# Split products for the attention and recurrence inputs of the second block's mixer

## The reference

```
x = x + 0.5 * swiglu(rms_norm_2(x, norm_ffn1[l]), ffn1_in[l], ffn1_out[l])
h = rms_norm_2(x, norm_mix[l])
proj = h @ w_in[l]
p_rwkv, p_attn, p_gate = split(proj, [C_RWKV, C_RWKV + C_ATTN])
o_a = rwkv7_mixer(p_rwkv, ...)          # C_RWKV = 1920 columns
o_b = diff_attention(p_attn, ...)       # C_ATTN = 1536 columns: q, k, v
merged = sum(sigmoid(p_gate) * [o_a @ w_branch[0], o_b @ w_branch[1]])
x = x + merged @ w_out[l]
x = x + 0.5 * swiglu(rms_norm_2(x, norm_ffn2[l]), ffn2_in[l], ffn2_out[l])
```

## Time and profile before

| | |
|---|---|
| median of 3 runs | 4137.35 us (4134.38 to 4137.35) |
| the profiled execution | 4137.76 us, of which the span from first to last instruction is 4136.1 us |
| PE | busy 3485.1 us, 84% of the span |
| DVE | 1569.9 us, 38% |
| ACT | 842.4 us, 20% |
| POOL | 599.4 us, 14% |
| mean granted clock of TensorE | 0.890 |

### The profile page before, as it was taken

How to read it: one execution, slowest core, us unless ns; L and a number is a source line. 1 busy time by engine, 2 the same in 40 slices (tenths; PEclk the granted TensorE clock), 3 DMA queues, 4 the chain that set the end, 5 groups by cost and what they waited for, 6 DMA issues and landing times.

```text
span 4136.1 us, 46292 instructions
## 1 busy us (share of the span) xinstructions
PE 3485.1 (84%) x18496; PEld 2414.5 (58%) x18496; DVE 1569.9 (38%) x2703; ACT 842.4 (20%) x1240; POOL 599.4 (14%) x556
## 2 busy tenths in 40 slices
PE   6888999994788899999299958798988994879899
PEld 3754333331566333333098648686978963877688
DVE  4433222224634222222354265531545426554154
ACT  1211111110130111111132221111324223111132
POOL 4402233331440233233100000000000000000000
PEclk8889999997878999999699968779998996877999
DMA  7647999985754899889554300004536430000352
GB/s 264 236 158 279 364 347 354 356 338 197 283 181 168 343 351 353 341 350 358 181 195 153 130 8 1 1 21 147 199 102 225 159 117 21 1 1 13 130 204 102
DMA packets 305420, 799.38 MB, mean 193 GB/s; under 512 B 57030, under 2 KB 155868, under 8 KB 251308
## 3 DMA queue, kind: packets, MB, share of 16 engines
q1 hardware_dynamic: 245804, 727.16, 46.8%
q0 software_dynamic: 58848, 67.05, 4.9%
q10 hardware_dynamic: 544, 2.10, 0.1%
HBM read 989.01 MB, written 53.48 MB: 252 GB/s over the span
## 4 chain that ended last, share of the span: by engine, by line
PE 41%; DVE 6%; ACT 1%; issue 1%; DMA 1%; SPq 0%; DVEq 0%
PE s_bank L1899 12%; PE s_bank L1937 6%; PE s_bank L1887 5%; PE s_bank L2083 2%; PE s_bank L1964 2%; PE s_bank L2098 2%; PE s_bank L2093 1%; PE s_bank L2200 1%; PE s_bank L2210 1%; PE s_bank L2168 1%; PE s_bank L2160 1%; PE s_bank L2071 1%; DMA s_ringA<-in_ffn_in 1%; PE s_bank L2153 1%; PE s_bank L2145 1%
## 5 line engine op out<-in xcount | busy, mean ns | idle before, releaser
L711 PE MATMUL f_bank<-f_ringA,f_arena 128*64 128x512 f32 x3072 | 688.7, 601 | 16.3 <-DMA f_ringA<-in_w_up,f_chosen 10.1
L711 PEld LDWEIGHTS f_bank<-f_ringA,f_arena 128*64 128x64 f32 x3072 | 222.3, 138 | 401.4 <-issue 400.1
L1899 PE MATMUL s_bank<-s_hT_high_parts,s_highA_parts 128*128 128x256 f32 x1408 | 402.7, 286 | 17.7 <-DVE s_hT_parts L2428 17.7
L1899 PE MATMUL s_bank<-s_hT_parts,s_highA_parts 128*128 128x256 f32 x1408 | 402.2, 286 | 0.0
L1899 PE MATMUL s_bank<-s_hT_high_parts,s_ringA_parts 128*128 128x256 f32 x1408 | 402.0, 285 | 0.0
L732 PE MATMUL f_bank<-f_ringB,f_arena 128*64 128x512 f32 x1536 | 346.5, 592 | 1.0 <-DVE f_arena L1473 1.0
L1012 ACT ACTIVATE f_arena<-f_bank 128x512 f32<-128x512 f32 (+1 forms) x362 | 202.1, 587 | 575.1 <-PE f_bank L692 174.2
L1465 DVE TENSOR_TENSOR f_arena<-f_arena,f_bank 128x256 f32<-128x256 f32 x96 | 58.6, 610 | 636.3 <-ACT f_arena L1090 636.3
L1899 PEld LDWEIGHTS s_bank<-s_hT_high_parts,s_highA_parts 128*128 128x128 f32 x1408 | 274.2, 195 | 20.4 <-issue 19.0
L1899 PEld LDWEIGHTS s_bank<-s_hT_parts,s_highA_parts 128*128 128x128 f32 x1408 | 274.3, 195 | 1.4
L1899 PEld LDWEIGHTS s_bank<-s_hT_high_parts,s_ringA_parts 128*128 128x128 f32 x1408 | 274.1, 195 | 0.0
(11 more groups left out here) (393 smaller groups left out, 5361.2 us busy)
## 6 DMA issues: line engine op xcount, KB each, us to landing
f_ringA<-in_w_gate SPq DMA_DIRECT2D x128, 1024.0 KB, 8.7
f_ringA<-in_w_up SPq DMA_DIRECT2D x128, 1024.0 KB, 11.1
f_ringB<-in_w_down SPq DMA_DIRECT2D x128, 1024.0 KB, 12.3
s_ringA<-in_ffn_in SPq DMA_DIRECT2D x88, 1024.0 KB, 7.7
f_ringA<-in_w_ada SPq DMA_DIRECT2D x48, 1024.0 KB, 8.4
s_arena<-in_ffn_out SPq DMA_DIRECT2D x44, 1024.0 KB, 6.0
s_ringA<-in_w_in SPq DMA_DIRECT2D x40, 1024.0 KB, 6.1
f_ringA<-in_w_in SPq DMA_DIRECT2D x28, 1024.0 KB, 10.2
```

Of the source, the lines that this page charges most:

```text
L711: last = mm(ps[j * CAP:(j + 1) * CAP, :].rearrange("p (h c) -> p h c", h=2), picked[:, b % 2, k, j * CAP:(j + 1) * CAP], gu[j][:, :, k, :] ...
L1899: last = mm(ps[:, t * S:(t + 1) * S], parts_of(wx[:, k, cs_]), parts_of(hx[:, k, :]), start=(k == 0 and x == 0), stop=(k == DT - 1 and x = ...
```

## The change

The attention and the recurrence input products of the mixer are formed from high and low parts in three products, in the manner of the feed-forward. The seven chunks that they read (MIX = 7) are copied by ACT (`mix_up`) into the two buffers of `highA` and reduced by DVE (`mix_down`). hT is split as well, with the low part in a place of its own, `hT_low`, since the gates' products still need hT whole. TensorE waits for `mix_low` instead of the landing of a chunk, and at the first product for `mix_split`, the four splits of hT.

```
+        hT_low = parts_of.part("hT_low", arena, arena_at, 20480, 2048).rearrange("p (t s) -> p t s", s=S)
...
+        def mix_chunk(c):
+            width = 512 if c < MIX - 1 else CRW - 1536
+            return [rows8(w)[:, :, 0:width] for w in (slotA(a_at + c), highA[:, (STEPS + c) % 2, :])]
...  TensorE
                 for c in range(3):
-                    landed(a_at + c)
-                    w = rows8(slotA(a_at + c))
+                    pe.wait_ge(mix_low, c + 1)
+                    w, high = mix_chunk(c)
                     for m in range(MT):
                         ps = banks.claim(pe, ("at", c, m))
                         for k in range(DT):
-                            last = mm(ps[:, :], hT[:, k, m * P:(m + 1) * P], w[:, k, :],
-                                      start=(k == 0), stop=(k == DT - 1))
+                            if c == m == 0 and k % 2 == 0:
+                                pe.wait_ge(mix_split, k // 2 + 1)
+                            for x, (hx, wx) in enumerate(((hT_high, high), (hT_low, high), (hT_high, w))):
+                                last = mm(ps[:, :], parts_of(hx[:, k, m * P:(m + 1) * P]), parts_of(wx[:, k, :]),
+                                          start=(k == 0 and x == 0), stop=(k == DT - 1 and x == 2))
                 for g in range(8):
-                    c = a_in + g // 2
                     if g % 2 == 0:
-                        landed(c)
...
+                        pe.wait_ge(mix_low, 3 + g // 2 + 1)
+                    w, high = mix_chunk(3 + g // 2)
...
+                        for k in range(DT):
+                            for x, (wx, hx) in enumerate(((high, hT_high), (high, hT_low), (w, hT_high))):
+                                last = mm(ps[:, t * S:(t + 1) * S], parts_of(wx[:, k, o:o + P]), parts_of(hx[:, k, :]),
...  ACT
+            def mix_up(c):
+                a_filled(act, a_at + c)
+                banks.read(act, ("u", 0, STEPS - 2 + c) if c < 2 else ("at", c - 2, 1) if c < 5 else ("rw", 2 * (c - 5) + 1))
+                w, high = mix_chunk(c)
+                f(parts_of(high), w, ACT.Copy).then_inc(mix_high, 1)
             def norm(k, at):
+                if k == 1:
+                    mix_up(0)
                 if k:
                     act.wait_ge(x_ready, k)
...
                 roots(MT)
+                if k == 1:
+                    mix_up(1)
...
                 for c in range(3):
                     for m in range(MT):
                         take(("at", c, m), at_tok[:, m, c * 512:(c + 1) * 512], lambda ps: ps[:, :])
+                    mix_up(c + 2)
                 act.wait_ge(lam_asked, 1)
...  in the loop over g
+                    if g in (1, 3):
+                        mix_up(5 + g // 2)
...  DVE
+                def mix_down(c):
+                    w, high = mix_chunk(c)
+                    dve.wait_ge(mix_high, c + 1)
+                    tt(parts_of(w), w, parts_of.value(high), ALU.subtract).then_inc(mix_low, 1)
```

More of the change, by code:

```diff
@@ L1640, in second_block @@
         lowB_ready, hT_split, hid_split = each["lowB_ready"], each["hT_split"], each["hid_split"]
+        mix_high, mix_low, mix_split = each["mix_high"], each["mix_low"], each["mix_split"]
         merged, dve_steps, arrived = each["merged"], each["dve_steps"], each["arrived"]
@@ L1963, in _ @@
                         for k in range(DT):
-                            last = mm(ps[:, :], hT[:, k, m * P:(m + 1) * P], w[:, k, :],
-                                      start=(k == 0), stop=(k == DT - 1))
+                            if c == m == 0 and k % 2 == 0:
[3 more added lines that the diff above has]
+                                          start=(k == 0 and x == 0), stop=(k == DT - 1 and x == 2))
                         banks.fill(last, ("at", c, m))
                 for g in range(8):
-                    c = a_in + g // 2
                     if g % 2 == 0:
-                        landed(c)
-                    w = rows8(slotA(c))
+                        pe.wait_ge(mix_low, 3 + g // 2 + 1)
+                    w, high = mix_chunk(3 + g // 2)
                     ps = banks.claim(pe, ("rw", g))
-                    o = (g % 2) * 2 * P
-                    banks.fill(hidden(ps, w[:, :, o:o + 2 * P], 1 if g == 7 else 2), ("rw", g))
+                    for t in range(1 if g == 7 else 2):
+                        o = (2 * (g % 2) + t) * P
+                        for k in range(DT):
+                            for x, (wx, hx) in enumerate(((high, hT_high), (high, hT_low), (w, hT_high))):
+                                last = mm(ps[:, t * S:(t + 1) * S], parts_of(wx[:, k, o:o + P]), parts_of(hx[:, k, :]),
+                                          start=(k == 0 and x == 0), stop=(k == DT - 1 and x == 2))
+                    banks.fill(last, ("rw", g))
                 pe.wait_ge(at_ready, 1)
@@ L2266, in norm @@
                         j = 2 * b + t
[L2267 to L2270 removed]
+                        f(hT[:, j, :], ps[:, t * S:(t + 1) * S], ACT.Copy, scale=cols[:, at + j:at + j + 1])
+                        last = f(parts_of(hT_high[:, j, :]), ps[:, t * S:(t + 1) * S], ACT.Copy,
+                                 scale=cols[:, at + j:at + j + 1])
                     banks.free(last, key)
@@ L2410, in norm @@
                         split_up(k, 0)
+                    else:
+                        mix_down(1)
                     if k == 0:
@@ L2417, in norm @@
                             j = 2 * b + t
-                            last = ts(hT[:, j, :], ps[:, t * S:(t + 1) * S], cols[:, at + j:at + j + 1], None,
-                                      ALU.mult)
-                            if k != 1:
-                                last = ts(parts_of(hT_high[:, j, :]), ps[:, t * S:(t + 1) * S],
-                                          cols[:, at + j:at + j + 1], None, ALU.mult)
-                        banks.free(last, key)
-                    if k != 1:
-                        for b in range(4):
-                            banks.evacuated(dve, ("xT", k, b))
-                            two = slice(2 * b, 2 * b + 2)
-                            tt(parts_of(hT[:, two, :]), hT[:, two, :], parts_of.value(hT_high[:, two, :]),
-                               ALU.subtract).then_inc(hT_split, 1)
+                            ts(hT[:, j, :], ps[:, t * S:(t + 1) * S], cols[:, at + j:at + j + 1], None,
+                               ALU.mult)
+                            last = ts(parts_of(hT_high[:, j, :]), ps[:, t * S:(t + 1) * S],
+                                      cols[:, at + j:at + j + 1], None, ALU.mult)
+                        banks.free(last, key)
+                    for b in range(4):
+                        banks.evacuated(dve, ("xT", k, b))
+                        two = slice(2 * b, 2 * b + 2)
+                        tt(parts_of((hT_low if k == 1 else hT)[:, two, :]), hT[:, two, :], parts_of.value(hT_high[:, two, :]),
+                           ALU.subtract).then_inc(mix_split if k == 1 else hT_split, 1)
                 def split_up(k, s):
@@ L2466, in ffn @@
                     dve.nop().then_inc(x_ready, 1)
+                    if k == 0:
+                        mix_down(0)
                 norm(0, r_ffn1)
```

13 lines of the change are left out of this document (9 added, 4 removed).

## The result

| | before | after |
|---|---|---|
| median (9 runs each) | 4137.35 us (4131.70 to 4143.09) | 4145.06 us (4142.64 to 4150.96) |
| profiled execution, its span | 4137.76, 4136.1 us | 4145.06, 4143.2 us |
| PE, DVE, ACT busy | 3485.1, 1569.9, 842.4 us | 3454.9, 1638.3, 892.0 us |
| mean granted clock | 0.890 | 0.886 |

The account below looks back on a forecast made before the run. TensorE bounds both product stages; the products' gain of 34.5 us is paid back by 12.2 at the start, 21.4 in the middle and 6.6 by the clock: +5.6 us, median 4143.0, range 4134 to 4149.

Parts of the forecast that it names:

- rival A: Whole kernel: the sum holds with its terms a microsecond or so off, 4139 to 4148 us; chance 62%.
- attention, 144 products: Mixer's attention stage: 48 products as three each, 32.8 us plus 2.0 for the half clock, before 42.87 and 41.44.
- middle wait: Between attention and recurrence, each layer: TensorE idle 10.7 us until the split of chunk 3, queued behind lambda, is done.
- recurrence, 360 products: Recurrence input stage, each layer: 120 products as three each, 43.15 us plus 2.0 for the half clock, before 51.81.
- The products: Attention and recurrence input, split products at 228 and 119.9 ns: 17.25 us a layer less, 34.5 for both.
- rival D: Attention and recurrence input: new products spaced by their columns alone, 12 us less in all, 4131 us; chance 3%.
- The start: From x_ready to first attention product: added splits and copy cost 6.0 us in layer 0, 6.2 in layer 1.
- Rival B: Between attention and recurrence: the wait is hidden by an earlier exponential, 25.4 us less, 4117.6 us; chance 5%.
- The half clock: Two product starts a layer behind idle gaps: clock at 0.50 costs 2.0 us each, bounds 0 and 2.2.
- Rival C: At the gaps: clock does not fall or is back in time, up to 8 us less, 4135 to 4139; chance 17%.
- The other chunks: Splits of chunks 2, 4, 5, 6: ready before TensorE needs them; chunk 5 tightest, 22.1 against 23.0 us.
- rival E: Recurrence, chunk 5: a second TensorE wait of about 3 us plus clock loss, 10 us more, 4153; chance 13%.

Follow-up runs that it names:

- the filled gap: Changed kernel plus 42 TensorE products, result never read, in the gap between attention and recurrence products; 4143.75 us, ratio 1.0016 to the kernel before.
- fillers: Version with lambda last and the start rearranged, plus 30 and 8 unread TensorE products in the scan's direction 0; 4113.02 us, ratio 0.9942.

## Why the prediction was right

Its number was 4143.0, the result 4145.06, inside 4134 to 4149, and rival A, the sum as it stands, is what happened. That the median came so close has some luck in it, too: the prediction did not know of the scan's two lengths, which differ by up to 10 us between two profiled executions and happened to be short in the profiled executions of both kernels. What does not rest on that luck are the stages, measured one by one:

| term | forecast | layer 0 | layer 1 |
|---|---|---|---|
| squares to first product | 16.6 us | 16.65 | 16.64 |
| attention, 144 products | 34.8 | 34.63 | 35.62 |
| middle wait | 10.7 | 10.63 | 10.64 |
| recurrence, 360 products | 45.15 | 46.17 | 45.18 |

**The products.** Away from the starts, the windows of the kernel after (columns as above) answer to the earlier trace rows:

```profile
2290.00:2319.40 29.40, 29.38 (x130) 24.01 (x128) 4.91 (x3) 10.03 (x7) 0.00 (x0) 1.00 0.41 143
2342.00:2376.00 34.00, 34.00 (x285) 34.00 (x285) 20.50 (x26) 14.12 (x20) 0.00 (x0) 1.00 0.49 170
```

29.38 us for 130 products are 226 ns each, 34.00 for 285 are 119.3, where the earlier trace rows gave 228 and 119.9. Products with a weight load each are as dear here as in the feed-forward, and rival D is out. The 216 and 109 ns of the Trainium skill's "TensorE: Matmul & The Clock Gate" ("Back-to-back issue gap") do not hold here. That section calls them the gap of an isolated matmul, which the prediction left out, and gives 131 ns for 512 columns in a stream of weight loads and matmuls; the measured 226 ns is farther from that than from the 216. (By the 216 and 109 ns the two stages would be 5.6 us a layer shorter, not 5.5 as the prediction has it.)

**The start.** Split, copy, split, scalings and splits of hT came in the order read from the earlier trace rows; the experiment on the start moved the two splits and the copy and got 4.2 us of the 6 back.

**The middle wait** was right to 0.1 us in both layers. Two experiments show that its terms are the right ones, not a sum that happens to fit: the split moved ahead of the lambda wait removes it, and the exponential moved ahead of the copy shortens it by the copy. Rival B, the wait hidden, is out.

**The half clock** is the term that was mis-sized. The prediction took 2.0 us a start from the feed-forward's 2.2 and 1.8. With the products at 228 and 119.9 ns the stages of the kernel after hold 1.8 + 3.0 us beyond them in layer 0 and 2.8 + 2.0 in layer 1: 4.8 a layer, 2.4 a start. That is 1.6 us over both layers, and, less 0.1 us of the middle wait, it is all by which the span's difference, 7.1 us, exceeds the forecast 5.6; the rest of the 2.1 us lies between the profiled executions and the medians. The bound of 2.2 was too narrow as well, since two starts cost 3.0 and 2.8. The clock behind the middle gap, layer 0 (windows, columns as above):

```profile
2328.00:2330.00 2.00, 0.00 (x0) 0.00 (x0) 2.00 (x2) 0.00 (x0) 0.00 (x0) 0.50 0.00 0
2330.10:2334.00 3.90, 3.90 (x18) 3.90 (x19) 3.87 (x3) 0.00 (x0) 0.00 (x0) 0.50 0.00 0
2334.00:2338.00 4.00, 4.00 (x28) 4.00 (x27) 3.96 (x3) 0.23 (x1) 0.00 (x0) 0.72 0.00 0
```

It stays at 0.50 for the first 3.9 us and for over half of the next four (0.72), where the earlier trace rows had shown only the first four of such a start. Rival C, no fall of the clock, is out, and the filled gap shows what it would have given in this stage: 2.7 and 1.7 us.

**The other chunks** came in time: no gap in 360 products, so rival E, a second wait at chunk 5, did not come. It was near, though. Chunk 5's split was done 23.8 us after the recurrence's start in layer 0 and 22.8 in layer 1, not 22.1, since DVE waited 1.90 and 0.96 us for ACT's copy, which the forecast's sum did not have. It was needed at 25.8 and 24.8: 2.0 us to spare. Once the middle gap is removed, chunk 4 is late by 3.87 us: the gap had given DVE the time that hid it. With chunk 4's split moved ahead as well, chunk 5 is late by 3.47, this time by ACT's copy behind the root.

**What was wrong**, beside the size of the half clock's term, were my expectations of the edits. I reckoned the splits on DVE and left out that ACT's next copy stands behind a root that waits for DVE, and I took what a stage gains for what the kernel gains, with a scan behind it that takes 164 or 169 us. That the scan took the rest is shown for the profiled executions only.

## What to carry to other kernels

Before a helper engine is put in front of TensorE, look for the longest wait that it already has: an idle of 45 us that cost nothing becomes TensorE's own wait as soon as work for TensorE is queued behind it. The cure was to move the waiting instructions (lambda: two small operations and an exponential) behind the work that TensorE needs. With the edit of the start, this gave more than moving the splits one by one (0.9929 against 0.9973); without it the ratios, 0.9975 and 0.9983, are too near each other to tell, but the profiles have 169.24 and 169.60 us to the scan against 173.79 and 175.10. And when an edit takes 25 us off its stages and the median falls by 17 (19 by the ratios), look for a stage behind it whose length has two values before looking for an error in the edit.

## What I had not expected of the hardware

- Direction 0 of the scan has two lengths, 164 and 169 us, apart by about 5 us; ten of 24 such stretches in the twelve profiles without fillers in it had the long one. In these stretches the granted clock rises either right behind the transposes or some 20 us later. The same kernel had it one way in layer 0 and the other in layer 1, and in its next profile the other way round. The profiled executions of before and after happened to have the short one in both layers, so the comparison of these two is free of it; of the other eight runs of each nothing shows it.
- A start of split products behind an idle TensorE cost 1.8 to 3.0 us in the kernel after, not 2.0 (the attention products took 34.23 to 35.80 us over all the runs, 1.4 to 3.0 beyond their 32.83). In the kernel after the attention's and the recurrence's surcharges came to 4.8 us in both layers, though not in equal parts.
- ACT's copy of 128x4096 floats and DVE's subtraction take 3.6 and 4.43 us also where both run at once (2320.92 and 2321.52 above): on these two operations the engines do not slow each other. The prediction had supposed this for the subtraction.
